# Multiplying output gates into weights on GpSimd instead of into results on VectorE

## The reference

```
mods = einsum('bd,lde->lbe', silu(c), ada_w) + ada_b[:, None, :]
shift, scale, gate = split(mods[m], 3, axis=-1)      # m = 0..3
h = rms_norm_2(x, gain) * (1 + scale) + shift
x = x + gate[:, None, :] * (hidden @ w_out)          # mixer or swiglu
```

## Time and profile before

| | us |
|---|---|
| median of 3 runs | 2118.65 |
| lowest, highest | 2115.97, 2118.83 |
| the profiled execution | 2115.04 |
| its span, first to last instruction | 2113.1 |
| TensorE busy | 2056.0 |
| VectorE busy | 1250.9 |
| ScalarE busy | 798.2 |
| GpSimd busy | 81.2 |

### The profile page before, as it was taken

The page is one execution under the profiler, slowest core; times in us unless marked ns, Lnnn a source line. Parts: engine busy times, 40 slices in busy tenths (PEclk is TensorE's granted clock), DMA queues, the critical chain, the costliest instruction groups (busy, mean ns, idle before and its releaser), DMA issues.

```text
span 2113.1 us, 31219 instructions
## 1 busy us (share of the span) xinstructions
PE 2056.0 (97%) x12286; PEld 1687.1 (80%) x12286; DVE 1250.9 (59%) x2209; ACT 798.2 (38%) x1455; POOL 81.2 (4%) x79
## 2 busy tenths in 40 slices
PE   8999899999999999999999999999899899999998
PEld 7687688888888877788888888779767688888887
DVE  5577767777645449746555546566776756322334
ACT  4323643333424552244222232433457733222222
POOL 1022000000000002000000000001001200000000
PEclk9999999999999999999999999999999999999999
DMA  6221025655433232213655645322300025233221
GB/s 211 80 80 61 21 90 182 197 179 180 159 129 100 80 100 79 66 35 99 203 172 184 200 135 189 100 85 81 120 2 2 2 80 176 83 100 100 100 90 50
DMA packets 146701, 231.51 MB, mean 110 GB/s; under 512 B 7325, under 2 KB 83709, under 8 KB 146557
## 3 DMA queue, kind: packets, MB, share of 16 engines
q1 hardware_dynamic: 144300, 224.05, 32.8%
q0 software_dynamic: 864, 3.15, 0.4%
q10 hardware_dynamic: 1392, 2.33, 0.3%
HBM read 227.41 MB, written 2.10 MB: 109 GB/s over the span
## 4 chain that ended last, share of the span: by engine, by line
PE 84%; DVE 9%; ACT 3%; issue 3%; DMA 0%; POOL 0%; DVEq 0%; POOLq 0%; ACTq 0%; SPq 0%
PE ps L2338 11%; PE ps L2340 11%; PE ps L2339 11%; PE ps L2583 4%; PE ps L2365 4%; PE ps L2367 4%; PE ps L2366 4%; PE ps L2290 4%; PE ps L2292 4%; PE ps L2291 4%; PE ps L2581 3%; PE ps L2656 3%; PE ps L2421 2%; PE ps L2386 2%; PE ps L2398 2%
## 5 line engine op out<-in xcount | busy, mean ns | idle before, releaser
L1595 DVE TENSOR_TENSOR w_lo<-ring,w_hi 128x1024 fp32r<-128x1024 f32 (+4 forms) x362 | 376.6, 1042 | 695.3 <-ACT w_hi L995 693.6
L995 ACT ACTIVATE w_hi<-ring 128x1024 fp32r<-128x1024 f32 (+4 forms) x362 | 329.4, 912 | 964.4 <-PE ps L2340 467.0
L2338 PE MATMUL ps<-x_hi,w_hi 128*128 128x512 f32 x1056 | 415.9, 394 | 0.0
L2340 PE MATMUL ps<-x_hi,w_lo 128*128 128x512 f32 x1056 | 411.2, 389 | 0.0
L2339 PE MATMUL ps<-x_lo,w_hi 128*128 128x512 f32 x1056 | 410.8, 389 | 0.0
L2339 PEld LDWEIGHTS ps<-x_lo,w_hi 128*128 128x128 f32 x1056 | 198.3, 188 | 42.4 <-issue 1.9
L2338 PEld LDWEIGHTS ps<-x_hi,w_hi 128*128 128x128 f32 x1056 | 198.3, 188 | 42.3 <-issue 1.9
L2340 PEld LDWEIGHTS ps<-x_hi,w_lo 128*128 128x128 f32 x1056 | 198.2, 188 | 41.9
L2365 PE MATMUL ps<-w_hi,x_hi 128*128 128x512 f32 x480 | 187.5, 391 | 3.6 <-DVE x_hi L1671 3.6
L2366 PE MATMUL ps<-w_lo,x_hi 128*128 128x512 f32 x480 | 186.8, 389 | 0.0
L2367 PE MATMUL ps<-w_hi,x_hi 128*128 128x512 f32 x480 | 186.8, 389 | 0.0
(11 more groups left out here) (346 smaller groups left out, 3010.8 us busy)
## 6 DMA issues: line engine op xcount, KB each, us to landing
ring<-in_ada_w SPq DMA_DIRECT2D x48, 1024.0 KB, 5.2
ring<-in_ffn_w_in SPq DMA_DIRECT2D x88, 512.0 KB, 4.4
ring<-in_w_up SPq DMA_DIRECT2D x44, 512.0 KB, 4.8
ring<-in_ffn_w_out SPq DMA_DIRECT2D x20, 1024.0 KB, 4.9
ring<-in_hgrn_w_in SPq DMA_DIRECT2D x16, 1024.0 KB, 5.2
ring<-in_w_in SPq DMA_DIRECT2D x12, 1024.0 KB, 5.1
ring<-in_w_down SPq DMA_DIRECT2D x10, 1024.0 KB, 4.9
ring<-in_kv_ada_w SPq DMA_DIRECT2D x8, 1024.0 KB, 5.0
```

What stands on the lines that cost most here:

```text
L995: a.activation(to[:, n % depth, 0:src.shape[-1]], src, ACT.Copy).then_inc(s["hi_done"], 1)
L1595: v.tensor_tensor(to[:, n % depth, 0:width], src, hi[:, n % depth, 0:width].bitcast(F32), ALU.subtract).then_inc(s["lo_done"], 1)
L2338: mm(bs[j], wh[:, k, c], x_hi[:, 2 * q + k], start=first, stop=False)
L2340: ins = mm(bs[j], wl[:, k, c], x_hi[:, 2 * q + k], start=False, stop=last)
```

## The change

The gate is multiplied into the weights of the product, not into the product. GpSimd waits until a half of a ring slot with weights of mix2, mix3 or of the down GEMMs of FFN 1 and 2 has landed (and until both halves of the gate row are made), multiplies each piece in place by the gate row (60 operations of 128x1024), and counts them in a new semaphore `w_gated`. ScalarE waits for the count before it makes the high part; VectorE's low part follows the high part as before. The results are added to `x_tok` straight from PSUM, and freeing the bank is what tells ScalarE that the part is there. The order on GpSimd: mix2's eight pieces after the HGRN gate products, FFN 1's 22 after the load of gate row 2, mix3's eight one by one behind the fifth to twelfth NSA sum, FFN 2's 22 at the end. Gate row 2 is loaded when mix2's eight pieces are multiplied, gate row 3 when FFN 1's are. The idle turns of norms 3, 4 and 5 are changed, and four idle turns stand before each ada unit's sums in `ada_columns`, in FFN 0 (two units) and in FFN 1 (four).

```diff
-            for n, (half, t) in enumerate(PARTS[-1]):
-                X_DONE[stage, t, half] = done + (n + 1 if stage >= 2 else t + 1)
-            STAGE_DONE.append(done + (2 * NT if stage >= 2 else NT))
+            if stage < 2:
+                for half, t in PARTS[-1]:
+                    X_DONE[stage, t, half] = done + t + 1
...
+        GATED = [("mix2", 0, u, q) for u in range(2) for q in range(4)] + [("down", 1, 1, k) for k in range(FT)] \
+            + [("mix3", 2, u, q) for u in range(2) for q in range(4)] + [("down", 3, 2, k) for k in range(FT)]
+        GATED_AT = {(name, i, k): n + 1 for n, (name, _, i, k) in enumerate(GATED)}
...
+            def gate_weights(some):
+                for name, m, i, k in some:
+                    for half in range(2):
+                        evacuated(pool, ("ada", m, 4 + half))
+                    gate = row[:, m % 2, :]
+                    if name == "down":
+                        g0 = next(n for n, (k0, _) in enumerate(down_groups) if k0 <= k < k0 + down_groups[n][1])
+                        k0, n = down_groups[g0]
+                        h, at = (k - k0) // (n // 2), (k - k0) % (n // 2)
+                        w = in_halves(arrived(pool, ("down", i, g0), (h,)), n // 2, PIECE)[:, h, at]
+                    else:
+                        w = arrived(pool, (name, i), (k // 2,))[:, k * PIECE:(k + 1) * PIECE].rearrange("p (k n) -> p k n", k=2)
+                        gate = gate[:, i * HALF:(i + 1) * HALF].unsqueeze(1).broadcast_to([P, 2, HALF])
+                    g.tensor_tensor(w, w, gate, ALU.mult).then_inc(s["w_gated"], 1)
             def load_gate(m):
 
-                pool.wait_ge(s["x_ready_v"], STAGE_DONE[m])
+                if m < 2:
+                    pool.wait_ge(s["x_ready_v"], STAGE_DONE[m])
+                else:
+                    pool.wait_ge(s["w_gated"], {2: 8, 3: 8 + FT}[m])
                 pool.dma_start(row[:, m % 2, :], io["ada_b_2"][m, 2 * D:3 * D].partition_broadcast(P)).then_inc(s[f"gate_row_in{m % 2}"], 16)
 
...
+            gate_weights(GATED[0:8])
             load_gate(2)
+            gate_weights(GATED[8:8 + FT])
             load_gate(3)
...
                 g.tensor_tensor(w, w, n_tmp[:, i % 2], ALU.add).then_inc(s["nsa_added"], 1)
+                if 4 <= i < 12:
+                    gate_weights(GATED[8 + FT + i - 4:8 + FT + i - 3])
+            gate_weights(GATED[16 + FT:])
...
-                act.wait_ge(s["x_ready_v"], X_DONE[stage, t, half])
+                if stage < 2:
+                    act.wait_ge(s["x_ready_v"], X_DONE[stage, t, half])
+                else:
+                    evacuated(act, part_key(stage, half, t))
...
+            def weight_gated(name, i, k):
+                if (name, i, k) in GATED_AT:
+                    act.wait_ge(s["w_gated"], GATED_AT[name, i, k])
...
+                weight_gated(name, i // 4, i % 4)
...
+                weight_gated("down", i, 0)
...
+                weight_gated("down", i, 1)
...
+                        weight_gated("down", i, k)
...
-                x_part_ready(5, t, 1)
+                for half in range(2):
+                    x_part_ready(5, t, half)
                 act.dma_start(out[0, t * P:(t + 1) * P, :], x_tok[:, t]).then_inc(s["out_done"], 16)
...
-            def gated(stage, m, half, t):
+            def part_added(stage, half, t):
 
                 key = part_key(stage, half, t)
                 p = filled(dve, key)
-                evacuated(dve, ("ada", m, 4 + half))
                 f = slice(half * HALF, (half + 1) * HALF)
-                v.tensor_tensor(STAGE_Y[stage][:, t, f], p, row[:, m % 2, f], ALU.mult).then_inc(free(key), 1)
-            def gated_added(stage, half, t):
-                evacuated(dve, part_key(stage, half, t))
-                f = slice(half * HALF, (half + 1) * HALF)
-                v.tensor_tensor(x_tok[:, t, f], x_tok[:, t, f], STAGE_Y[stage][:, t, f], ALU.add).then_inc(s["x_ready_v"], 1)
-            def post_gate(stage, m):
+                v.tensor_tensor(x_tok[:, t, f], x_tok[:, t, f], p, ALU.add).then_inc(free(key), 1)
+            def post_gate(stage):
 
                 i = stage + 1
                 if i == 4:
                     early_lows(i, slice(0, 3))
                 if stage in HALF_FIRST:
                     for t in range(NT):
-                        gated(stage, m, 0, t)
-                        if t:
-                            gated_added(stage, 0, t - 1)
-                    gated_added(stage, 0, NT - 1)
+                        part_added(stage, 0, t)
                 for t in range(NT):
-                    if stage in HALF_FIRST:
-                        gated(stage, m, 1, t)
-                        gated_added(stage, 1, t)
-                    else:
-                        gated(stage, m, 0, t)
-                        gated(stage, m, 1, t)
-                        gated_added(stage, 0, t)
-                        gated_added(stage, 1, t)
+                    if stage not in HALF_FIRST:
+                        part_added(stage, 0, t)
+                    part_added(stage, 1, t)
                     if t and stage < 5:
                         x_normed(i, t - 1)
                 if stage == 3:
...
-            BUSY = {0: (15, 0, 0, 0), 1: (0, 36, 0, 0), 2: (0, 36, 0, 0), 3: (0, 13, 7, 0), 4: (0, 0, 0, 13), 5: (0, 13, 7, 0)}
+            BUSY = {0: (15, 0, 0, 0), 1: (0, 36, 0, 0), 2: (0, 36, 0, 0), 3: (0, 8, 4, 0), 4: (0, 0, 4, 0), 5: (0, 8, 4, 0)}
...
+                        keep_busy(b, 4, 1)
```

More of the change, by code:

```diff
@@ L168, in build @@
             tables_done whole_done hi_done lo_done piece_done x_split hid_hi acc_done gate_row_in0 gate_row_in1
-            acc_half zero_done keys_zero k_shifted rk_shifted x0_hi x0_split kv_staged x4_hi x4_split out_hi cmp_zero x_ready_v""".split()
+            acc_half zero_done keys_zero k_shifted rk_shifted x0_hi x0_split kv_staged x4_hi x4_split out_hi cmp_zero x_ready_v w_gated""".split()
         s = {n: sem(n) for n in names}
@@ L713, in build @@
             done = STAGE_DONE[-1] if STAGE_DONE else 0
-            for n, (half, t) in enumerate(PARTS[-1]):
-                X_DONE[stage, t, half] = done + (n + 1 if stage >= 2 else t + 1)
-            STAGE_DONE.append(done + (2 * NT if stage >= 2 else NT))
+            if stage < 2:
+                for half, t in PARTS[-1]:
+                    X_DONE[stage, t, half] = done + t + 1
+                STAGE_DONE.append(done + NT)
         def part_key(stage, half, t):
@@ L2001, in _ @@
                 out_weight("mix2", i)
-            post_gate(2, 0)
+            post_gate(2)
             norm(3)
             ffn(1)
-            post_gate(3, 1)
+            post_gate(3)
             norm(4)
@@ L2209, in _ @@
             out_parts(2, "mix3")
-            post_gate(4, 2)
+            post_gate(4)
             norm(5)
             ffn(2)
-            post_gate(5, 3)
+            post_gate(5)
         @block.tensor
```

## The result

The changed kernel takes 2140.28 us (median of 4 runs, 2135.94 to 2140.87) against 2118.42 for the kernel before: a ratio of 1.0105, 95% interval 1.0093 to 1.0117. It is slower by 22 us. Its profiled execution took 2135.94 us (span 2134.1), that of before 2115.04 (span 2113.1), so the traces have 20.9 us of this between them and the rest is the distance of each profiled execution from its median.

A forecast was written before the change was run, and what follows sets the result against it. TensorE, busy 97% of the span, was taken as the bound. 20.6 + 0.3 + 1.3 - 6.1 = +16.1 us gave 2131.1 on the profiled execution, 2134.8 on the median; forecast 2133, range 2112 to 2140.

The forecast's parts named there:

- the hold: A VectorE operation with two SBUF inputs waits 2.2 us for a 128x1024 GpSimd multiplication (bounds 1.1 and 2.4).
- FFN 1's down GEMM: Held low parts and ada sums delay TensorE: 5.2, then 13.2 over three groups, then 2.2; +20.6 us (bounds 0 to 23).
- the term for mix2: HGRN stage: first three pairs of halves absorbed by VectorE's gaps, the fourth partly; +1.3 us (bounds 0 and 4.4).
- ada terms are held: FFN 1's down GEMM: two GpSimd operations hold each ada sum, 4.4 us; without this the sum is 4 x 4.4 = 17.6 smaller.
- sign of 4 us of idle TensorE: FFN 1's down GEMM: TensorE idle about 4 us before pieces 5, 9, 13 and 17 if the forecast is right.
- Norms 3 and 5: Fewer VectorE multiplications at the hand-over, TensorE's queue late next: 1.3 us gained in each (bounds 0.4 to 2.3).
- the last stage: End of the program: one addition after the last bank instead of two multiplications and two additions; 1.6 us gained.
- norm 4: Hand-over after FFN 1: 3.1 us gained if the clock stays up, about 1.1 if it falls; 2.6 taken.
- FFN 2's down GEMM: No ada sums; only one hidden row's low part waits 2.2 us, 2.0 spare: +0.3 us (bounds 0 to 10).
- (1): Holds don't reach TensorE, so only the hand-overs count, with 0.5 of contention: 2113 us; chance 0.16.
- (2): One GpSimd operation per pair is seen, contention halves: 2121 us, about no change; chance 0.18.
- (3): Idle turns fail and the clock falls in norm 4, 3 or 5: up to +7 more, 2140 us; chance 0.11.

The follow-up runs named there:

- e1: The changed kernel with all 60 GpSimd multiplications narrowed from 1024 to 8 columns, waits and order kept: 2109.37 us, ratio 0.9964 to the kernel before.
- e10: The changed kernel with the 28 ada terms in FFN 1's down GEMM narrowed from 512 to 8 columns, GpSimd's multiplications whole: 2120.89 us, ratio 1.0019.
- e9: The changed kernel with GpSimd's multiplications at full width only for mix2's first six pieces, all others narrowed to 8 columns: 2113.85 us, ratio 0.9984.
- e3: The changed kernel with each of GpSimd's 60 multiplications replaced by a copy of the same 128x1024 floats onto themselves: 2116.75 us, ratio 0.9995.
- e4: The changed kernel with each of GpSimd's 60 multiplications issued as two operations on 512 columns each: 2138.44 us, ratio 1.0101.
- e2: The changed kernel with GpSimd's full-width multiplications kept only for mix2 and mix3, the 44 of the down weights narrowed to 8 columns: 2114.85 us, ratio 0.9988.
- e7: The changed kernel with the multiplications of mix2 and both down GEMMs moved to VectorE, and all idle turns as before: 2112.71 us, ratio 0.9981.
- e8: The kernel before with only the idle turns of norms 3, 4 and 5 moved, gates and hand-overs unchanged: 2116.71 us, ratio 0.9998.
- e11: The changed kernel with mix2's and both down GEMMs' multiplications on VectorE, and the idle turns of before at norms 4 and 2: 2111.12 us, ratio 0.9965.

## Why the prediction was right or wrong

The direction, the hold and its way to TensorE in FFN 1's down GEMM were right; the term for mix2 was not, and the clock's part had no term. The forecast of 2133 was 7 us low, and 2140.28 lies just above the range. On the profiled execution the sum gave 2131.1 and 2135.94 was measured, so 4.8 us is missing in the steps. The rest is in the base: the profiled executions lie 3.4 and 4.3 us under their medians, and I put the forecast between.

- **The hold.** Taken: 2.2 us, from a doubled 1.10. Measured: 2.88 - 0.68 = 2.20 (HGRN) and 2.86 - 0.68 in the down GEMM, and half of it for half the columns. That ada terms are held, which no row showed, was taken by what they read. Two terms of each sum are held, for 1.95 us each (2.7 for 0.75), so seven took 3.9 us more where 4.4 was taken. The Trainium skill (SBUF — State Buffer, SBUF: two separate sides) states the lock for a VectorE operation with two SBUF inputs only against a GpSimd operation that reads SBUF, and the copy's 0.84 us and the multiplication's 2.20 agree with it. The Trainium skill (GPSIMD Engine Reference, 3.1 Elementwise) has 2.6 cycles an element at 1.2 GHz for two inputs, from which 1024 elements are estimated at 2.22 us, beside the 2.20 measured.
- **FFN 1's down GEMM.** 20.6 predicted, 21.1 measured, and that they are so close is partly luck. Up to the fifth piece the lag grew by 4.4 us (5.2 worked out), then by 4.4, 4.2 and 6.1 in three groups (4.4 each, with 2.2 more for the last halves): 19.1 by the seventeenth piece, for 20.6. The other 2.0 come behind it, while the clock is at its lower level, which the sum did not have. The groups take 26.75, 26.55 and 28.5 us, for 26.65 worked out. Its sign of 4 us of idle TensorE before pieces 5, 9, 13 and 17 showed only before the last; the others are split, 1.5 to 2 us before pieces 3, 7, 11 and 15 and 0.7, 0.7 and 2.3 before 5, 9 and 13. That the holds cause the loss, and nearly all of it together with the ada terms, is shown by e1 and e10.
- **The failed step: mix2.** "the first three are absorbed by VectorE's 1.0 us gaps per 3.6 us", and of the fourth 3.1 of 4.4 us find a gap: +1.3. Measured: +4.6, of which 2.3 at the first three pairs (e9: 2.4), put at nothing, and 2.5 at the fourth, put at 1.3. My reading, argued and not shown by itself: a hold of 2.2 us reaches TensorE before gaps of 1.0 us have paid it back, so of each pair about 0.8 us stays. The upper bound of 4.4 had counted the fourth pair alone. The copy's smaller hold, 0.84 us, did disappear in the same gaps (e3: 0.0), and with the products in halves, holds of 1.1, the first three pairs left 0.3 (e4). So the prediction's absorption holds for a delay about as long as the gap, and not for one of twice the gap.
- **mix2's GEMM, not in the sum: +1.6.** In the changed kernel the granted clock falls to 0.5 (1.2 GHz) for 3.4 us from 938.7, which it doesn't in the trace of before (its clock is 1.00 from 933 to 936, at the same matmuls). The same happens in every kernel in which GpSimd gates six or more mix2 pieces at full width (e2, e4, e9, e10), but also in e7, where it does not. What sets it off stays open.
- **The hand-overs.** Norms 3 and 5 gave 1.6 and 1.7 for 1.3 each, the last stage 1.4 for 1.6. For norm 4, 2.6 stood between 3.1 with the clock up and 1.1 with it down; 3.4 was measured with the clock up. e8 shows that the turns alone give it; e7 had 4.0 from the hand-over alone in the execution in which the clock stayed up.
- **FFN 2's down GEMM.** +1.0 for +0.3, inside its bounds. Of 23 low parts of weights 13 keep their length of 1.23 us and ten take 1.61 to 2.63; of 19 of hidden rows two take 2.88 and 2.89 for 0.68; ScalarE once waited 3.8 us for a gated piece.
- **The rivals.** (1), holds that don't reach TensorE, would have been 2113; e1 shows what it meant, 2109. (2), half the contention, is excluded by a full 2.2 us on each of two operations a pair. (3), the clock falling in norm 3, 4 or 5, didn't happen in the changed kernel, though its neighbours show that it can in norm 4. It fell elsewhere: in mix2's GEMM and three times in FFN 1's down GEMM.
- **Slips in the working.** 26.65 - 22.4 is 4.25, counted as 4.4 in three groups, and 1261.1 - 1256.0 is 5.1, counted as 5.2; the sum would be 0.5 less. The 4.8 us from the GEMM's last matmul to norm 3's last tile are 981.57 - 976.95 = 4.6, on which nothing rests.

## What to carry to other kernels

Before moving elementwise work from VectorE to GpSimd, look at what VectorE does in the same stretch: operations with two SBUF inputs stand still while GpSimd reads, here 2.2 us for a 128x1024 product that VectorE makes in 1.2. If VectorE has idle time at all, put the product there, in the gaps, and far enough ahead of who reads it. When you ask whether a delay is absorbed, compare one whole delay with one gap, not the sums: 0.84 us went into gaps of 1.0 us without a trace, and pairs of 2.2 left 0.7 to 0.8 us a pair. Look at the granted clock of a stage too before its lag is put down to waits: 5 of the 21 us here came while it was at 1.2 GHz, which no kernel had without GpSimd's full-width products in that GEMM.

## What the runs showed of the hardware

- VectorE's operations with one input in PSUM are not held. All 44 of this form in the changed kernel's FFN 1 and 2 lie within 15 ns, six of them beside a GpSimd multiplication:

```profile
L1653 DVE TENSOR_TENSOR arena<-arena,ps x44: 674/680/689, 1020.1 to 2013.1; 128x512 f32<-128x512 f32 x44
```

- GpSimd's product is longer too where the two meet: 2.35 us at the least, 3.39 at the most (ns: shortest, median, longest):

```profile
L807 POOL TENSOR_TENSOR ring<-ring,row x60: 2354/2420/3390, 847.2 to 2091.4; 128x1024 f32<-128x1024 f32 x60
```

- The same instructions at the same place (norm 4 in e7 and e11) ran once at the upper and once at the lower level of TensorE's clock, 3.3 us apart. A difference of this size in a single trace can be such a fall; the clock of the stretch says so at once.
